# Seven-product feed-forward stage of a hybrid decoder layer: sample columns gated inside the PSUM bank, four down banks in the loops, casts and first sums reordered, output pieces moved to groups 19 and 20

## Chip, cores and metric

One core of a Trainium2 chip runs the whole kernel. The metric is device time in microseconds (us); lower is better. The kernel before takes 2521.41 us (median of 3 runs, 2520.0 to 2522.43).

Names of engines: PE is TensorE (matmuls), PEld its weight loads, DVE is VectorE, ACT is ScalarE, POOL is GpSimd, SP is SyncE, which issues most DMAs. L826 is line 826 of the kernel before.

## The reference

One decoder layer for 1024 prompt tokens and 64 sample tokens (8 sequences of 8), D_MODEL 1024, D_FF 2816, float32:

```python
x = x + 0.5 * gt1 * swiglu(modulate(x, norm_ffn1, sh1, sc1), ffn1_w_gu, ffn1_w_down)
x = x + gt2 * (parallel_heads(modulate(x, norm_mix, sh2, sc2)) @ w_out)
x = x + 0.5 * gt3 * swiglu(modulate(x, norm_ffn2, sh3, sc3), ffn2_w_gu, ffn2_w_down)
y = rms_norm(x, norm_final)
# swiglu(h, w_gu, w_down): gate, up = split(h @ w_gu, 2); (silu(gate) * up) @ w_down
```

The gates gt1 to gt3 have one value per channel for the prompt and one per channel and sequence for the samples. The change concerns the third line and the final norm.

## The kernel before

x stays in SBUF with channels on the partitions: 8 chunks of 128 channels by 1088 tokens, of which columns 1024 to 1087 are the samples. Each float32 product is made of three matmul passes over a high and a low part: high is the operand cast to fp32r (ACT), low is the operand less its high part (POOL or DVE). The last stage, `block_ffn` (L1510 to L2281), does the second feed-forward block. It works in two passes q over the tokens: tokens 0 to 543 (q = 0) and tokens 544 to 1087 (q = 1). A pass is two token tiles of 272 columns; the very last tile holds the 64 sample columns behind 208 prompt columns. Each pass goes over D_FF in 11 groups of two units (f chunks of 128 gate and 128 up channels), so groups are numbered G = 0 to 10 and 11 to 21.

The up and gate projections of a unit are a 2 by 2 block product done with seven block products in place of eight (named p1, p5, p6, p3, p7, p2, p4 in order of issue). Each product is 12 matmuls of 272 columns (L1802 to L1804) into PSUM banks 0 to 3. The weights need four sums of blocks first: S3 and S1 on POOL (L1679, L1685), S2 and S4 on DVE (L2085, L2091). Then ACT casts the high parts in two pieces (`up_high`, L1935, 2048 and 1536 columns) and POOL subtracts to get the low parts (`up_low`, L1690, four and three instructions of 512 columns). The x blocks have their sums too (T1 to T4), made once per pass.

After the products of a unit, DVE adds them up (`sum12`, `sum22`, `sum11`, L2095 to L2116), ACT applies silu (L1912 for the second token half, L1918 for the first), DVE multiplies (L2126, L2133), ACT casts the high part of the activation (`high`, L1922), DVE subtracts for its low part (`low`, L2121). Both units of a group being ready, PE does 16 down tiles v (8 output chunks for the second token half, v = 0 to 7, then 8 for the first, v = 8 to 15), 6 matmuls each (L487 to L489, called from `down`, L1807). A down tile goes to a bank of 4, 5, 6 in turn, and its wait on `dn_free` is for the DVE having read the tile three places before. DVE adds each tile to x with the gate (`summed`, L2144, which calls `add_gated_to`, L821):

```python
ins = dve.scalar_tensor_tensor(x[:, a:a + np_], bank[:, 0:np_], gate[:, 0:1], x[:, a:a + np_], ALU.mult, ALU.add)
if np_ < n:
    ins = dve.tensor_tensor(per_seq(scratch), per_seq(bank[:, np_:n]), over_tokens(gate[:, 1:9]), ALU.mult)
    dve.drain()
    dve.tensor_tensor(x[:, NP_TOK:T], x[:, NP_TOK:T], scratch, ALU.add)
```

The caller puts the increment of `dn_free` on the returned instruction. Only tiles v = 0 to 7 of pass q = 1 have sample columns. Among the tiles DVE also does S2 (after v = 8) and S4 (after v = 10) of the next group's second unit; S2 and S4 of its first unit stand between the two units (L2148).

Order of work is what each engine's program says: all five have a loop over groups and wait on one another's semaphores. ACT's `group` (L1941) does, for the second unit: take p1, silu, `up_high(G+1, 0, 0)`, high of the second half, silu, `up_high(G+1, 0, 1)`, high of the first half, then `up_high(G+1, 1, 0)` and `(1, 1)`. POOL's `group` does `up_lows(G, 1)`, S3, `dn_low(G)` (L1697, four instructions), S1, S3, `up_lows(G+1, 0)`, S1. SP's `next_group` (L1624) loads the next group's blocks as the products free them, and the down weights (1 MB) once the last down tile is through.

Before the first group, `first_sums` (DVE L2187, POOL L1724) and `first_highs` (ACT L1961) make the T sums and the high and low parts of the seven x blocks. In group 0 PE also takes the means of squares of the second pass's norm between down tiles (`early_means`, after v = 4, 7, 10, 13), for which ACT makes the squares (L764).

The final norm and output are cut into ten pieces of tokens (`Outputs`, L835). Per piece: PE transposes 8 blocks into two PSUM banks (L868), ACT squares and sums (L898), takes the root (L902, L904), DVE takes the reciprocal (L934), DVE scales and weights one half of the row (L942), ACT scales the other half (L930), POOL weights it (L954), SP writes it out. Pieces 0 to 3 (tokens 0 to 511, final since the first pass) use banks 4 to 7 and are all placed in group 21, after the second and sixth product of each unit. Before the down tiles of group 21 PE waits for these banks (L1893 to L1895).

## Time and profile before

| what | value |
|---|---|
| median of 3 runs | 2521.41 us |
| profiled execution, its own time | 2511.55 us |
| its span, first to last instruction | 2509.8 us |
| mean granted clock of TensorE | 0.979 |
| PE / PEld / DVE / ACT / POOL busy | 94% / 88% / 53% / 26% / 41% |
| `block_ffn`, first product to end of span | 1636.9 to 2509.8 us |
| a group of the first pass's loop (G = 1 to 9) | about 34.9 us |
| a group of the second pass's loop (G = 12 to 20) | about 37.8 us |
| group 0, group 10, group 11 (take of p1 to next) | 50.4, 51.3, 40.1 us |

The profiled execution lies 9.86 us below the median of the three runs. Busy time of PE comes from modelled ends of pipelined matmuls, so it is start-to-start steps and the idle times in brackets that show lost time.

### The profile page before, as it was taken

The page shows a single profiled execution, that of the slowest core. Times are in us where ns is not written, and L with a number is a line of the kernel's source. Part 1 is how long each engine was busy: PE and PEld are TensorE (multiplying, and loading weights), DVE is VectorE, ACT ScalarE, POOL GpSimd, SP SyncE. Part 2 cuts the span into 40 slices and gives each one's busy share as a digit, 9 for nine tenths or more (in the row PEclk, how much of TensorE's full clock was granted, in tenths as well). Part 3 has the DMA queues.
Part 4 walks back from the last instruction along what each step waited for, and adds up shares of the span by engine and source line. Part 5 has one row for each costly group of instructions (what it writes and reads, how often), then busy time and mean ns, then how long its engine had stood idle before and what let it go on. Part 6 is the DMA issues. An engine that isn't in the chain of part 4 may idle for free. (4 is left out here: it accounts for less than half of the span.)

```text
span 2509.8 us, 55182 instructions
## 1 busy us (share of the span) xinstructions
PE 2351.6 (94%) x22802; PEld 2209.7 (88%) x22802; DVE 1319.6 (53%) x2888; ACT 662.2 (26%) x1198; POOL 1032.9 (41%) x732
## 2 busy tenths in 40 slices
PE   6999999999999999999898899969999989999996
PEld 5899999999999999888488867969999978988986
DVE  4634444333444545343876752365656686666664
ACT  4100000000000323344611131254344343333335
POOL 2312121121221121111612044277878888778773
PEclk9999999999999999999899999989999999999998
DMA  9223221111101231011400025113322222322322
GB/s 331 85 101 100 67 84 51 50 47 37 50 21 46 72 95 56 26 35 39 140 4 5 5 64 154 44 51 101 92 87 87 85 76 76 92 75 84 92 70 86
DMA packets 214396, 185.91 MB, mean 74 GB/s; under 512 B 23787, under 2 KB 193436, under 8 KB 213843
## 3 DMA queue, kind: packets, MB, share of 16 engines
q1 hardware_dynamic: 213714, 181.36, 23.2%
q8 instruction: 122, 2.00, 0.3%
q10 hardware_dynamic: 144, 2.23, 0.2%
q14 instruction: 32, 0.25, 0.0%
q0 software_dynamic: 384, 0.07, 0.0%
HBM read 172.58 MB, written 11.34 MB: 73 GB/s over the span
## 5 line engine op out<-in xcount | busy, mean ns | idle before, releaser
L1690 POOL TENSOR_TENSOR f_up_lo<-f_up_raw,f_up_hi 128x512 fp32r<-128x512 f32 x308 | 392.8, 1312 | 146.8 <-ACT f_up_hi L1935 146.8
L487 PE MATMUL bank<-f_a_hi,f_dn_hi 128*128 128x272 f32 (+2 forms) x1232 | 393.4, 319 | 40.8 <-DVE f_scratch L829 20.8
L1802 PE MATMUL bank<-f_x_hi,f_up_hi 128*128 128x272 f32 x1232 | 361.9, 294 | 21.9 <-DVE f_x_lo L2162 10.3
L489 PE MATMUL bank<-f_a_hi,f_dn_lo 128*128 128x272 f32 (+2 forms) x1232 | 377.3, 306 | 0.0
L488 PE MATMUL bank<-f_a_lo,f_dn_hi 128*128 128x272 f32 (+2 forms) x1232 | 376.9, 306 | 0.0
L1804 PE MATMUL bank<-f_x_hi,f_up_lo 128*128 128x272 f32 x1232 | 359.3, 292 | 0.0
L1803 PE MATMUL bank<-f_x_lo,f_up_hi 128*128 128x272 f32 x1232 | 357.6, 290 | 0.0
L487 PE MATMUL bank<-hh,f_up_hi 128*128 128x368 f32 (+1 forms) x1008 | 331.0, 328 | 0.0
L489 PE MATMUL bank<-hh,f_up_lo 128*128 128x368 f32 (+1 forms) x1008 | 329.5, 327 | 0.0
L488 PE MATMUL bank<-hl,f_up_hi 128*128 128x368 f32 (+1 forms) x1008 | 329.1, 326 | 0.0
L487 PEld LDWEIGHTS bank<-f_a_hi,f_dn_hi 128*128 128x128 f32 x1232 | 233.3, 189 | 68.3 <-DVE f_scratch L829 33.3
L1101 POOL TENSOR_TENSOR f_up_lo<-f_up_raw,f_up_hi 128x2048 fp32r<-128x2048 f32 x22 | 101.8, 4626 | 408.1 <-DVE f_up_hi L1357 408.1
L1802 PEld LDWEIGHTS bank<-f_x_hi,f_up_hi 128*128 128x128 f32 x1232 | 234.8, 191 | 25.6 <-issue 13.4
L1370 DVE TENSOR_TENSOR f_prod<-f_silu,bank 128x368 f32<-128x368 f32 (+1 forms) x66 | 35.2, 533 | 394.4 <-PE bank L489 388.3
L1803 PEld LDWEIGHTS bank<-f_x_lo,f_up_hi 128*128 128x128 f32 x1232 | 235.3, 191 | 0.0
L1804 PEld LDWEIGHTS bank<-f_x_hi,f_up_lo 128*128 128x128 f32 x1232 | 234.7, 191 | 0.0
L488 PEld LDWEIGHTS bank<-f_a_lo,f_dn_hi 128*128 128x128 f32 x1232 | 234.0, 190 | 0.0
L489 PEld LDWEIGHTS bank<-f_a_hi,f_dn_lo 128*128 128x128 f32 x1232 | 233.6, 190 | 0.0
L502 DVE SCALAR_TENSOR_TENSOR x<-bank,mods,x 128x368 f32<-128x368 f32 (+1 forms) x280 | 157.8, 573 | 136.8 <-PE bank L489 124.7
L1306 ACT ACTIVATE f_silu<-bank 128x368 f32<-128x368 f32 (+1 forms) x66 | 31.3, 474 | 722.2 <-PE bank L489 717.2
L1935 ACT CAST f_up_hi<-f_up_raw 128x2048 fp32r<-128x2048 f32 x88 | 146.3, 1690 | 250.4 <-DVE f_up_raw L2091 228.2
L487 PEld LDWEIGHTS bank<-hh,f_up_hi 128*128 128x128 f32 x1008 | 189.1, 188 | 4.9 <-issue 4.9
(456 smaller groups left out, 4778.6 us busy)
## 6 DMA issues: line engine op xcount, KB each, us to landing
f_dn_raw<-in_ffn_w_down SPq DMA_DIRECT2D x33, 1024.0 KB, 4.9
f_up_raw<-in_ffn_w_gu SPq DMA_DIRECT2D x132, 256.0 KB, 2.9
f_up_raw<-in_ffn_w_gu SPq DMA_DIRECT2D x44, 512.0 KB, 5.0
ada<-in_w_ada SPq DMA_DIRECT2D x12, 1024.0 KB, 17.0
late<-in_w_ada SPq DMA_DIRECT2D x12, 1024.0 KB, 4.7
f_up_tmp<-in_ffn_w_gu SPq DMA_DIRECT2D x42, 256.0 KB, 3.8
w_in_raw<-in_w_in SPq DMA_DIRECT2D x16, 512.0 KB
gates<-in_w_ada SPq DMA_DIRECT2D x8, 1024.0 KB, 6.8
```

What stands on the lines that cost most here:

```text
L487: pe.matmul(out, wh, rh, start=(n == 0), stop=False)
L488: pe.matmul(out, wh, rl, start=False, stop=False)
L489: ins = pe.matmul(out, wl, rh, start=False, stop=(n == last))
L502: ins = dve.scalar_tensor_tensor(x[:, a:a + np_], bank[:, 0:np_], gate[:, 0:1], x[:, a:a + np_], ALU.mult, ALU.add)
L1101: pool.tensor_tensor(up_lo[j][:], up_raw[:], up_hi[j][:].bitcast(F32), ALU.subtract).then_inc(up_lo_done, 1)
L1306: act.activation(silu[u % 2][:, 0:n], k.psum[2 * (u % 2)][:, 0:n], ACT.Silu).then_inc(gate_free, 1)
L1370: dve.tensor_tensor(prod[u % 2][:, 0:n], silu[u % 2][:, 0:n], k.psum[2 * (u % 2) + 1][:, 0:n], ALU.mult).then_inc(up_free, 1)
L1690: ins = pool.tensor_tensor(up_lo[j][:, at], up_raw[j][:, at], up_hi[j][:, at].bitcast(F32), ALU.subtract)
L1802: pe.matmul(out, up_hi[j][:, w], x_hi[:, x], start=(c == 0), stop=False)
L1803: pe.matmul(out, up_hi[j][:, w], x_lo[:, x], start=False, stop=False)
L1804: ins = pe.matmul(out, up_lo[j][:, w], x_hi[:, x], start=False, stop=(c == KH - 1))
L1935: act.copy(up_hi[j][:, PARTS[part]], up_raw[j][:, PARTS[part]]).then_inc(up_hi_done[part], 1)
```

## The change

- `add_gated_to`: for a tile with sample columns, DVE first multiplies the 64 columns by their gates in place in the bank, then adds the 208 prompt columns to x, drains, and adds the 64 columns from the bank to x. The increment of `dn_free` is on this last instruction. The scratch tensor is no longer used here.
- Down tiles use four banks (4 to 7) in groups 1 to 9 and 11 to 20; three in groups 0, 10 and for v < 11 of group 21, then two.
- ACT's `group` casts the high part of the second half right after its silu and product, ahead of `up_high(G+1, 0, 0)`.
- Start of group 0: T3 and the low parts of B22 and B21 go from POOL to DVE; DVE's S2 and S4 of unit 1 go ahead of T1; ACT's order of casts changes and `take_p1(0, 0)` goes behind them. The last squares of the second pass's norm go ahead of `up_high(1, 1, ·)`.
- Output pieces 0 to 3: two in group 19 and two in group 20, one per unit, transposed after the second product. PE waits at the start of each of the two groups for all its down tiles to have been read, and before the down tiles of each for the rows of both pieces. ACT does a piece's squares and root after the high part of the unit's first half, DVE scales it there as well. Group 21 has no pieces in its products. In its down tiles DVE scales pieces 4, 5, 6 after v = 12, 14, 15 (was 11, 13, 15).
- SP issues the load of the final norm's weight ahead of the second pass's loads, not behind them.

```diff
-def add_gated_to(dve, k, i_gate, c, tile, bank, scratch):
+def add_gated_to(dve, k, i_gate, c, tile, bank):
...
+    if np_ < n:
+        dve.tensor_tensor(per_seq(bank[:, np_:n]), per_seq(bank[:, np_:n]), over_tokens(gate[:, 1:9]), ALU.mult)
     ins = dve.scalar_tensor_tensor(x[:, a:a + np_], bank[:, 0:np_], gate[:, 0:1], x[:, a:a + np_], ALU.mult, ALU.add)
     if np_ < n:
-
-        ins = dve.tensor_tensor(per_seq(scratch), per_seq(bank[:, np_:n]), over_tokens(gate[:, 1:9]), ALU.mult)
         dve.drain()
-        dve.tensor_tensor(x[:, NP_TOK:T], x[:, NP_TOK:T], scratch, ALU.add)
+        ins = dve.tensor_tensor(x[:, NP_TOK:T], x[:, NP_TOK:T], bank[:, np_:n], ALU.add)
...
-    def down_bank(v, last):
-        return k.psum[4 + (v % 2 if last and v >= KD else v % 3)]
+    def down_bank(v, banks):
+        return k.psum[4 + (v + 1) % 2] if banks == 2 else k.psum[4 + v % banks]
...
+            for sem in (sum_t1, sum_t3):
+                sp.wait_ge(sem, 2)
+            sp.dma_start(outputs.weight[:], ...
             with sp.Fori(0, NGRP - 1) as g:
                 next_group(g + NGRP, g + 1)
...
-            first_sums()
             with pool.Fori(0, NGRP - 1) as g:
                 group(g)
...
-                if last and v >= KD:
-                    pe.wait_ge(dn_free, ND * G + v - 1)
-                elif v >= 3:
-                    pe.wait_ge(dn_free, ND * G + v - 2)
+                if v >= banks:
+                    pe.wait_ge(dn_free, ND * G + v - banks + 1)
...
-            with pe.Fori(NGRP + 1, 2 * NGRP - 1) as g:
+            with pe.Fori(NGRP + 1, 2 * NGRP - 3) as g:
                 group(g)
+            for G in (2 * NGRP - 3, 2 * NGRP - 2):
+                pe.wait_ge(dn_free, ND * G)
+                for j in range(FC):
+                    for i in range(7):
+                        product(G, j, i)
+                        if i == 1:
+                            outputs.pe_tile(pe, FC * (G - 2 * NGRP + 3) + j)
+                outputs.set_free(pe, FC * (G - 2 * NGRP + 3) + 2, True)
+                for v in range(ND):
+                    down(G, v)
             G = 2 * NGRP - 1
-            pe.wait_ge(dn_free, ND * G)
...
-                    if i in (1, 5):
-                        outputs.pe_tile(pe, 2 * j + i // 5)
-            outputs.set_free(pe, 4)
-            pe.wait_ge(outputs.rows_done, outputs.EARLY)
-            pe.wait_ge(outputs.act_scaled, outputs.EARLY)
             for v in range(ND):
-                down(G, v, True)
+                down(G, v, 3 if v < KD + 3 else 2)
...
                 take_p1(G, 1)
-                swish2(G, 1)
+                second(G, 1)
                 up_high(G + 1, 0, 0)
-                high(G, 1, 1, gated2, high2)
                 swish1(G, 1)
...
                 if j == 0:
                     norms[1].squares(act, 2, 1)
                     norms[1].squares(act, 3, 0)
-            norms[1].squares(act, 3, 1)
+                    norms[1].squares(act, 3, 1)
...
+            for G in (2 * NGRP - 3, 2 * NGRP - 2):
+                n = FC * (G - 2 * NGRP + 3)
+                take_p1(G, 0)
+                second(G, 0)
+                dn_high(G)
+                first(G, 0)
+                outputs.squares(act, n)
+                take_p1(G, 1)
+                outputs.half_scale(act, n, outputs.bank(n, 0))
+                second(G, 1)
+                up_high(G + 1, 0, 0)
+                swish1(G, 1)
+                up_high(G + 1, 0, 1)
+                high(G, 1, 0, gated1, high1)
+                outputs.squares(act, n + 1)
+                outputs.half_scale(act, n + 1, outputs.bank(n + 1, 0))
...
             def first_sums():
...
+                sum_s2(0, 1)
+                sum_s4(1)
                 dve.wait_ge(norms[0].h_done, 2 * KD)
...
-                sum_s2(0, 1)
-                sum_s4(1)
+                x_low(X_B22, b22)
+                dve.tensor_tensor(t3, b22, b12_, ALU.subtract).then_inc(sum_t3, 1)
+                x_low(X_T3, t3)
+                x_low(X_B21, b21)
                 x_low(X_T4, t4)
...
+            for G in (2 * NGRP - 3, 2 * NGRP - 2):
+                for j in range(FC):
...
+                    low(G, j, 0, high1, act1_done)
+                    outputs.scaled(dve, FC * (G - 2 * NGRP + 3) + j)
+                    if j == 0:
+                        sum_s2(G + 1, 0)
+                        sum_s4(0)
```

## Rows read from the trace of the kernel before

**Rows 1.** The page: busy time of each engine and its share of the span.
```profile
PE 2351.6 (94%) x22802; PEld 2209.7 (88%) x22802; DVE 1319.6 (53%) x2888; ACT 662.2 (26%) x1198; POOL 1032.9 (41%) x732
```
**Rows 2.** Stretches: full clock, half clock, first-pass group, second-pass group; PE, PEld, DVE, ACT, POOL, PEclk.
```profile
2104.20:2116.20 12.00, 12.00 (x97) 12.00 (x97) 4.93 (x12) 3.79 (x7) 10.64 (x10) 1.00 0.55 178
2476.80:2479.80 3.00, 3.00 (x14) 3.00 (x15) 0.92 (x4) 0.00 (x0) 0.92 (x1) 0.50 0.27 77
1768.86:1803.73 34.87, 34.13 (x266) 33.43 (x266) 21.23 (x42) 14.45 (x17) 28.49 (x23) 1.00 0.30 91
2141.89:2179.72 37.83, 35.62 (x267) 33.73 (x266) 24.87 (x58) 11.89 (x15) 28.42 (x23) 1.00 0.27 82
```
**Rows 3.** PE's timeline, down tiles of group 12: start, duration, idle before and its releaser.
```profile
2123.78 0.39 PE L487 MATMUL bank<-f_a_hi,f_dn_hi 128*128 128x272 f32 x1 [0.16 <-issue]
...
2128.48 0.40 PE L487 MATMUL bank<-f_a_hi,f_dn_hi 128*128 128x272 f32 x1 [0.76 <-DVE f_scratch L829]
```
**Rows 4.** DVE's timeline, sample tiles v = 0, 1 and 5 of group 12.
```profile
2126.10 0.42 DVE L826 SCALAR_TENSOR_TENSOR x<-bank,mods,x 128x208 f32<-128x208 f32 x1
2126.44 0.21 DVE L829 TENSOR_TENSOR f_scratch<-bank,mods 128x64 f32<-128x64 f32 x1
2126.75 1.21 DVE L831 TENSOR_TENSOR x<-x,f_scratch 128x64 f32<-128x64 f32 x1
...
2128.52 0.67 DVE L831 TENSOR_TENSOR x<-x,f_scratch 128x64 f32<-128x64 f32 x1
...
2133.48 0.23 DVE L831 TENSOR_TENSOR x<-x,f_scratch 128x64 f32<-128x64 f32 x1
```
**Rows 5.** POOL's timeline in group 12: low parts, S1, and dn_low with its idle time.
```profile
2113.66 5.93 POOL L1697 TENSOR_TENSOR f_dn_lo<-f_dn_raw,f_dn_hi 128x512 fp32r<-128x512 f32 x4 [1.36 <-ACT f_dn_hi L1939]
...
2122.86 8.72 POOL L1690 TENSOR_TENSOR f_up_lo<-f_up_raw,f_up_hi 128x512 fp32r<-128x512 f32 x7 [0.77 <-ACT f_up_hi L1935]
2131.54 1.29 POOL L1685 TENSOR_TENSOR f_up_raw<-f_up_raw,f_up_tmp 128x512 f32<-128x512 f32 x1
```
**Rows 6.** DVE adds with one operand in a bank: nanoseconds, minimum/median/maximum of 44.
```profile
L2110 DVE TENSOR_TENSOR f_u2s<-f_u2s,bank x44: 428/430/433, 1658.1 to 2466.6; 128x272 f32<-128x272 f32 x44
```
**Rows 7.** DVE's second-half product in group 12, then ACT's timeline behind it.
```profile
2121.51 0.45 DVE L2126 TENSOR_TENSOR bank<-bank,f_vs 128x272 f32<-128x272 f32 x1
...
2120.87 1.91 ACT L1935 CAST f_up_hi<-f_up_raw 128x2048 fp32r<-128x2048 f32 x1 [0.60 <-POOL f_up_raw L1685]
2123.63 0.40 ACT L1918 ACTIVATE bank<-f_p1s 128x272 f32<-128x272 f32 x1 [0.57 <-DVE f_a_lo L2121]
```
**Rows 8.** What PE waited for between 1725 and 2010 (G = 2 to 9): us, times, longest.
```profile
PE bank L487 <- DVE x L826: 4.5, 16, 0.4
```
**Rows 9.** PE's timeline at the start of group 0 and at its last means of squares.
```profile
1636.88 0.56 PE L1802 MATMUL bank<-f_x_hi,f_up_hi 128*128 128x272 f32 x1 [5.60 <-DVE f_x_lo L2162]
...
1654.63 0.57 PE L1802 MATMUL bank<-f_x_hi,f_up_hi 128*128 128x272 f32 x1 [5.17 <-issue]
...
1691.69 0.57 PE L774 MATMUL bank<-f_sq,const 128*32 128x68 f32 x12 [6.22 <-ACT f_sq L764]
```
**Rows 10.** DVE's timeline at the start of group 0: one low part of an x block.
```profile
1643.71 1.28 DVE L2162 TENSOR_TENSOR f_x_lo<-f_x_raw,f_x_hi 128x1088 fp32r<-128x1088 f32 x1
```
**Rows 11.** PE's timeline of group 21: first product, third piece's transposes, first down tile.
```profile
2444.01 0.39 PE L1802 MATMUL bank<-f_x_hi,f_up_hi 128*128 128x272 f32 x1 [0.59 <-DVE x L826]
...
2460.59 1.06 PE L868 MATMUL bank<-const,x 128*128 128x128 f32 x8 [0.94 <-ACT x L930]
...
2476.54 0.59 PE L487 MATMUL bank<-f_a_hi,f_dn_hi 128*128 128x272 f32 x1 [6.46 <-DVE x L942]
```
**Rows 12.** The fourth output piece in group 21: ACT's squares and table load, DVE's scaling.
```profile
2472.18 0.60 ACT L898 ACTIVATE x<-bank 128x512 f32<-128x512 f32 x1
...
2473.86 1.28 ACT L904 ACT_TABLE_LOAD   x1
...
2475.74 0.75 DVE L942 SCALAR_TENSOR_TENSOR x<-bank,y_sums,y_weight 128x512 f32<-128x512 f32 x1
```

More of the change, by code:

```diff
@@ L869, in turn, with set_free @@
         return ins
-    def set_free(self, pe, j):
-        before = [i for i in range(j) if self.SETS[i] == self.SETS[j]]
+    def set_free(self, pe, j, every=False):
+        before = [i for i in range(j) if every or self.SETS[i] == self.SETS[j]]
         if before:
@@ L1655, in _ @@
             next_group(NGRP - 1, 0)
-            with sp.Fori(0, NGRP - 1) as g:
-                next_group(g + NGRP, g + 1)
             for sem in (sum_t1, sum_t3):
@@ L1661, in _ @@
                          ).then_inc(outputs.weight_in, 16)
+            with sp.Fori(0, NGRP - 1) as g:
+                next_group(g + NGRP, g + 1)
             outputs.sync(sp)
@@ L1805, in product, with down @@
                 ins.then_inc(prod_done[i], 1)
-            def down(G, v, last=False):
+            def down(G, v, banks=4):
                 a = SH * (1 - v // KD)
@@ L1820, in down @@
                 c = v % KD
-                three_passes(pe, down_bank(v, last)[:, 0:SH],
+                three_passes(pe, down_bank(v, banks)[:, 0:SH],
                              [(dn_hi[:, f, P * c:P * c + P], dn_lo[:, f, P * c:P * c + P], a_hi[:, f, a:a + SH], a_lo[:, f, a:a + SH])
@@ L1855, in early_means @@
                 for v in range(ND):
-                    down(0, v)
+                    down(0, v, 3)
                     if v in (4, 7, 10, 13):
@@ L2142, in unit, with summed, group @@
                 low(G, j, 0, high1, act1_done)
-            def summed(G, q, v, last=False):
+            def summed(G, q, v, banks=4):
                 dve.wait_ge(dn_mm, ND * G + v + 1)
-                return add_gated_to(dve, k, i_gate, v % KD, down_tile(q, v), down_bank(v, last), scratch[:, v % 2]).then_inc(dn_free, 1)
-            def group(G, q):
+                return add_gated_to(dve, k, i_gate, v % KD, down_tile(q, v), down_bank(v, banks)).then_inc(dn_free, 1)
+            def group(G, q, banks=4):
                 unit(G, 0)
@@ L2153, in group @@
                 for v in range(ND):
-                    summed(G, q, v)
+                    summed(G, q, v, banks)
                     if v == 8:
```

88 lines of the change are left out of this document (34 added, 54 removed).

## The prediction

> **What bounds the kernel now.** I read the page first: PE is busy 94% of the span and no other engine over 53% [rows 1]. So an edit pays only where PE's matmuls start late. The table of stretches gives the measure. At full clock 12.00 us hold some 95 starts, 0.126 us each; at a granted clock of 0.50 (1.2 of 2.4 GHz) 3.00 us hold 13, 0.23 each [rows 2]. A group has 14 x 12 + 16 x 6 = 264 matmuls, so its floor is 264 x 0.126 = 33.3 us. The first pass's loop takes 34.87 us, the second's 37.83 [rows 2]: 1.6 and 4.5 us lost per group. PE's timeline shows the losses at the down tiles: v = 0 starts 0.45 us behind its predecessor (0.16 idle and the predecessor's 0.29) where 0.126 is normal, so 0.3; then v = 4 idles 0.76 us for a DVE read of its bank [rows 3]. Each such late start costs 0.1 more, since its weight load isn't hidden. The sample tiles v = 0 to 7 are the second pass's extra.
>
> DVE's timeline says why [rows 4]. A sample tile is L826 (0.42), L829 (0.21), L831 (64 columns). L831 takes 1.21 and 0.67 us while POOL makes low parts, and 0.23 after. It reads two SBUF tensors; POOL's seven instructions take 8.72 / 7 = 1.25 us each [rows 5], and the first tiles come one per POOL instruction: L831 to L831 is 2128.52 - 2126.75 = 1.77, later ones 1.24. An add with one operand in a bank takes 428 to 433 ns in all 44 cases, beside POOL or not [rows 6]. So L831 waits for POOL's use of SBUF, and a bank operand frees it.
>
> **1. The sample tile, four banks, high part first (groups 11 to 18).** New tile: product in the bank, 0.14 to the next start (L829's 0.21 less the usual overlap of 0.07), L826's 0.42, drain 0.09 (L829 ends 2126.65, L831 starts 2126.75), add, 0.14 to the next start: 0.14 + 0.42 + 0.09 + 0.14 = 0.80 us against PE's 6 x 0.126 = 0.757. The add isn't in the trace; its bounds are 0.21 (L829, one bank operand) and 1.21 (L831 at worst). I take 0.21, since rows 6 show no waiting in this form. A page would have it dearer: the Trainium skill, "VectorE: DVE Perf Modes", section "The TRN2 errata", charges a bank source 120 cycles against 58, 65 ns more, by an estimate 0.93 us a tile and some 1 us more a group, 8 us in all. L829, from a bank, at 0.21 against L831 alone, from SBUF, at 0.23 shows no such surcharge [rows 4].
>
> The ACT move: the second half's product ends at 2121.96 [rows 7], so the high part starts at 2122.0, not behind the cast at 2122.7, and the first down tile needn't wait: 0.3 + 0.1 won. But the 1.91 us cast, which ran from 2120.87, now runs from 2122.3 to 2124.2; silu of the first half, at 2123.63, comes at 2124.1, and with it the second cast, the first half's high and low parts and DVE's first down tile: 2126.10 becomes 2126.55. PE's first tile starts at 2123.46; its fifth (v = 4) is due at 2126.49 and waits for the new release at the end of the add, 2126.55 + 0.14 + 0.42 + 0.09 + 0.21 = 2127.41: 1.0 + 0.1 lost. Then PE follows DVE's 0.80 to 0.81 for eight tiles: 8 x 0.05 = 0.4. POOL's low parts shift by 1.4 us with the cast and end, with S1's 1.29 [rows 5], near 2134.2, so DVE's S2 now falls beside POOL and v = 13 waits about 0.6. Loss 1.1 + 0.4 + 0.6 = 2.1 (bounds 1.3 and 3.0) against 4.5: -2.3 each (rounded), 8 x 2.3 = **-18** (-12 to -26). POOL waits 1.36 us for ACT before dn_low [rows 5] and starts about 0.85 later relative to the next group, so this cover just holds.
>
> **2. First pass (groups 1 to 9).** No sample tiles. The wait for DVE's read, 4.5 us in 16 cases over 8 groups [rows 8], is 0.56 a group, 0.76 with two late starts' extra. v = 4 is due at +3.03 and DVE comes 0.45 later than before, so that first wait stays at about 0.6; the one behind S2 goes, but S4 may now meet POOL. With v = 0's 0.4 won: -0.5 each (-0.2 to -0.9), 9 groups: **-4.5** (-2 to -8).
>
> **3. Start of group 0.** PE idles 5.6 us for the first low part and 5.17 us for T3's at 1654.63 [rows 9]. DVE gets three more instructions of 1088 columns, 1.28 us alone [rows 10], and POOL goes straight to the low weights. Two sums first (1.4 us, in an idle stretch of 0.8) delay T1 by 0.7, but without POOL beside them T1 and its successors take 1.28 to 1.3 each. I get the first product at 1636.4 and T3's low part at 1649 after alternating with four POOL instructions; `take_p1` after the casts lets p7 start at 1650, p2 waits for DVE's sum until 1652.5. That is **-3.7** (-1 to -5.5) at the group's seventh product. SP's down load waits for B21's low part, which DVE ends before T4's, at about 1650: ahead of p7's old start, so it isn't later, and the blocks queued behind it on SP aren't either. I take the point where p7 starts, less half of what p2's wait gives back; the low end is a first low part that only moves by the 0.5 us of the first product, the high end all of 5.17.
>
> **4. The last squares.** PE waited 6.22 us at 1691.69 [rows 9] and did its next 16 matmul steps at half clock (1.6 us). PE had come at 1691.69 - 6.22 = 1685.5. The squares need only the previous means, three down tiles earlier (3 x 0.757 + 0.1 = 2.4: 1683.1), and take ACT 1.1 us, so they are there by 1684.3. Next late is p1's copy, behind the roots' and a table load: 0.6. So -(6.22 + 0.3 + 1.6 - 0.6) = **-7.5** (-6 to -8.3).
>
> **5. Output pieces.** In group 21 go: the wait at the start (0.59 idle, 0.85 with restarts [rows 11]), 0.94 + 0.1 for piece 2's banks, 6.46 + 0.2 before the down tiles and 17 half-clock steps (17 x 0.1 = 1.8), in all 10.4. In come about 1.1, as DVE's first tile now lags. Transposes (0.95 a piece) move and cancel. In each of groups 19 and 20 come: 0.85 at the start; then piece n's squares and root, 3.3 us on ACT (table load 1.28 [rows 12]), hold DVE, which waits for the root before S2 and S4 of the next group, and these stand ahead of `sum12` of the second unit: p2 starts 1.9 late. After the unit's last high part ACT takes piece n + 1: 3.3, then DVE's reciprocal and 0.75 [rows 12], and PE's down tiles are held until both are done: from its first square to the end of that scaling the fourth piece took 2475.74 + 0.75 - 2472.18 = 4.3 us, and the high part ahead of it ends 2.4 us behind the products, so 6.7. The clock falls as it did after 6.46: 1.8. The tiles then have no backlog, 0.3. Sum 0.85 + 1.9 + 6.7 + 1.8 + 0.3 = 11.6 in place of 4.5: +7.1, twice +14.2. Net 14.2 - 10.4 + 1.1 = **+5** (-8 to +11; the low end if piece n + 1 hides). Table loads: the Trainium skill, "ScalarE: Activation LUTs", section "What ACT_TABLE_LOAD costs", adds a drain of 1.38 us to the load's 1.28. By it each group would lose 2.8 more, +5.5 in all. In rows 12 the root follows the load at once, so the sum leaves it out.
>
> **6. Rest.** The last group's fifth piece now pays a table load in the tail: **+0.8** (0 to 1.5). SP's weight load moves ahead of the loop: its waits are over before the first block is due, and 0.5 MB (the down load has 1 MB) finds the queue free: nothing; without this cover 1 to 2 us once.
>
> **Sum.** -18 - 4.5 - 3.7 - 7.5 + 5 + 0.8 = -27.9. Against the profiled execution 2511.55 becomes 2483.6; it lay 9.9 below the median of the runs, so against 2521.4 I expect **2493.5**.
>
> **Rivals.** (a) *The pieces hide*: ACT's last root comes before PE needs the banks. For it: PE needs only banks, and the transposes are 10 us earlier. Against: ACT's program has the squares behind the unit's last cast. It would save (6.7 + 1.8 - 1.4 for the backlog that returns) x 2 = 14: 2479. Chance 0.12.
> (b) *The add still waits for POOL*: x is in SBUF in both forms. Against: rows 6. Tiles stay at 1.24 and release the bank later; I work out -0.5 a group in place of -2.3: +14, 2508. Chance 0.12.
> (c) *Part 3 and 4's waits pass on* to POOL's low weights of the next unit, which follow their own casts: +9, 2502. Chance 0.1.
> (d) *Slower: the delayed cast chain becomes the bound.* Cast, low parts, S3, dn_low, S1 follow one another; the cast now starts 1.4 us later. dn_low ends at 2119.6 [rows 5], 4 us ahead of PE's tile at 2123.8, and POOL has 1.36 before it. Beyond 5.5 us of shift every down stage of 17 loop groups waits. A shift of 8 us costs 17 x 2.5 = 42: 2536. The row gives 1.4, so 0.04.
> (e) *The change doesn't do what it says*: the release behind the drain eats the fourth bank and pieces cost more, all parts cancelling: 2520. Chance 0.05.
>
> **Numbers.** The forecast has 0.57, its own range 2485 to 2502. 2479 to 2508 takes in (c), and the edges of (a) and (b). A measurement of this kernel can tell about 0.2%, 5 us, from no change: faster is the forecast and (a), (b), (c), 0.91; same is (e) 0.05; slower is (d) 0.04.
>
> **What would show it.** Right: L831's successor near 0.22 us at every tile; sample tiles 0.80 apart; second-pass groups near 35.5 us, first-pass 34.4; no PE wait over 1 us at the last means; PE idle near 6.5 us before the down tiles of both 19 and 20, with clock 0.5 behind it; group 21 without. Wrong: adds of 0.6 to 1.2 us (b); groups 19 and 20 under 40 us (a); PE waiting for dn_low (d).

## The result and the profile after

The changed kernel takes 2482.24 us (median of 4 runs, 2478.93 to 2486.84), the kernel before 2520.7 us beside it (4 runs, 2516.77 to 2522.43): 0.985 of the time, 95% interval 0.983 to 0.987. 2493.5 us were forecast, 2479 to 2508 the range. The profiled executions, 2511.55 and 2482.93 us, lie 28.6 us apart, for which 27.9 were forecast; the medians lie 38.5 apart, and the last experiment looks into why. One execution of the kernel of run 7, which took 2851.98 us at a mean granted clock of 0.745 where the others had 0.977 to 0.984, is left out of its median.

The page of the changed kernel, busy time by engine, beside [rows 1]:

```profile
PE 2331.9 (94%) x22802; PEld 2206.0 (89%) x22802; DVE 1294.8 (52%) x2891; ACT 665.2 (27%) x1202; POOL 1030.9 (42%) x726
```

The shares of busy time hardly move, though the kernel is 1.5% faster. The table of stretches shows where it gained: a first-pass group (G6), a second-pass group (G12), group 19, and the tail from the fifth output piece's transposes to the end. Columns as in [rows 2].

```profile
1859.55:1893.58 34.03, 33.56 (x267) 33.34 (x266) 20.24 (x42) 14.34 (x18) 29.48 (x23) 1.00 0.31 93
2082.75:2118.61 35.86, 34.23 (x266) 33.53 (x265) 23.73 (x58) 11.66 (x16) 28.48 (x23) 1.00 0.30 89
2334.48:2379.77 45.29, 37.07 (x282) 36.41 (x281) 23.69 (x62) 20.45 (x32) 28.02 (x23) 0.92 0.23 70
2453.23:2481.00 27.77, 13.21 (x86) 11.97 (x84) 11.38 (x23) 15.05 (x41) 6.92 (x5) 0.66 0.30 86
```

34.87 us have become 34.03 and 37.83 have become 35.86 [rows 2]; as means of several groups, 35.03 have become 34.13 and 37.92 have become 35.87. DVE's timeline of a sample tile in group 12, and the add's view by line (nanoseconds, minimum/median/maximum), beside [rows 4]:

```profile
2105.47 0.22 DVE L826 TENSOR_TENSOR bank<-bank,mods 128x64 f32<-128x64 f32 x1
2105.60 0.42 DVE L827 SCALAR_TENSOR_TENSOR x<-bank,mods,x 128x208 f32<-128x208 f32 x1
2106.09 0.22 DVE L830 TENSOR_TENSOR x<-x,bank 128x64 f32<-128x64 f32 x1
...
L830 DVE TENSOR_TENSOR x<-x,bank x88: 220/221/223, 2070.2 to 2452.8; 128x64 f32<-128x64 f32 x88
```

All 88 adds take 0.22 us, where L831 took 1.21 and 0.67 beside GpSimd; tiles start 0.76 to 0.78 apart. PE's remaining late starts in group 12 are two, v = 4 and one behind S2 (PE's timeline, then ACT's and POOL's, beside [rows 3, 5, 7]):

```profile
2106.37 0.39 PE L487 MATMUL bank<-f_a_hi,f_dn_hi 128*128 128x272 f32 x1 [0.92 <-DVE x L830]
...
2114.20 0.39 PE L487 MATMUL bank<-f_a_hi,f_dn_hi 128*128 128x272 f32 x1 [0.66 <-DVE x L827]
```
```profile
2100.90 0.39 ACT L1907 CAST f_a_hi<-bank 128x272 fp32r<-128x272 f32 x1 [0.85 <-DVE bank L2120]
2101.19 1.92 ACT L1920 CAST f_up_hi<-f_up_raw 128x2048 fp32r<-128x2048 f32 x1
```
```profile
2103.18 8.77 POOL L1686 TENSOR_TENSOR f_up_lo<-f_up_raw,f_up_hi 128x512 fp32r<-128x512 f32 x7 [2.54 <-ACT f_up_hi L1920]
2111.89 1.30 POOL L1681 TENSOR_TENSOR f_up_raw<-f_up_raw,f_up_tmp 128x512 f32<-128x512 f32 x1
```

GpSimd waits 2.54 us for the later cast, its S1 comes at 2111.89, and VectorE's S2 at 2112.05 takes 1.69 us beside it.

PE's timeline at the start of group 0, behind the last means, in group 19 and in the tail, beside [rows 9, 11]:

```profile
1638.18 0.56 PE L1785 MATMUL bank<-f_x_hi,f_up_hi 128*128 128x272 f32 x1 [4.92 <-DVE f_x_lo L2156]
...
1651.43 0.36 PE L1785 MATMUL bank<-f_x_hi,f_up_hi 128*128 128x272 f32 x1 [3.03 <-DVE f_x_lo L2156]
...
1654.76 0.36 PE L1785 MATMUL bank<-f_x_hi,f_up_hi 128*128 128x272 f32 x1 [1.58 <-DVE f_vs L2095]
...
1691.38 0.36 PE L1785 MATMUL bank<-f_x_hi,f_up_hi 128*128 128x272 f32 x1 [0.55 <-ACT f_p1s L1893]
...
2353.57 0.39 PE L1785 MATMUL bank<-f_x_hi,f_up_hi 128*128 128x272 f32 x1 [0.73 <-DVE f_vs L2095]
...
2363.75 0.59 PE L487 MATMUL bank<-f_a_hi,f_dn_hi 128*128 128x272 f32 x1 [6.89 <-DVE x L941]
...
2462.33 1.06 PE L867 MATMUL bank<-const,x 128*104 128x128 f32 x4 [1.78 <-DVE y_rows L941]
...
2466.54 0.84 PE L867 MATMUL bank<-const,x 128*96 128x128 f32 x3 [1.78 <-DVE y_rows L941]
```

The 6.22 us at the last means are gone (the 0.55 us are p1's copy of group 1); groups 19 and 20 each idle 6.9 us before their down tiles, as forecast, and the tail has two waits of 1.78 us where PE's timeline before had one:

```profile
2496.58 1.92 PE L868 MATMUL bank<-const,x 128*96 128x128 f32 x16 [1.78 <-DVE y_rows L942]
```

**How the experiments are read.** Ahead of VectorE's first product of the first norm (`xhat`) no instruction differs between any of the kernels here, yet it started between 1612.4 and 1625.7 us in the fourteen profiles. So beside the medians I give, from each profile, the time from that instruction to the end of the span, the *stage*: 896.4 us before, 865.6 after. "Second pass" is the mean of groups 12 to 17, "first pass" of groups 2 to 8, from p1's copy to the next group's; single groups of one kernel differ by steps of 0.4 to 0.5 us. Every ratio is to the kernel before, with its 95% interval.

### The profile page after: what moved, and what is told of

Its sections match the earlier page's. It is cut to its first block and busy times, and to the rows that moved or that the text cites. A ratio compares the mean times of both kernels' runs of the same rounds, so it can differ in the third digit from the quotient of the medians.

```text
span 2481.0 us, 55050 instructions
## 1 busy us (share of the span) xinstructions
PE 2331.9 (94%) x22802; PEld 2206.0 (89%) x22802; DVE 1294.8 (52%) x2891; ACT 665.2 (27%) x1202; POOL 1030.9 (42%) x726
## 5 line engine op out<-in xcount | busy, mean ns | idle before, releaser
L1686 POOL TENSOR_TENSOR f_up_lo<-f_up_raw,f_up_hi 128x512 fp32r<-128x512 f32 x308 | 401.2, 1342 | 151.3 <-ACT f_up_hi L1920 151.3
L487 PE MATMUL bank<-f_a_hi,f_dn_hi 128*128 128x272 f32 (+2 forms) x1232 | 384.9, 312 | 35.2 <-DVE x L941 13.8
L1785 PEld LDWEIGHTS bank<-f_x_hi,f_up_hi 128*128 128x128 f32 x1232 | 233.5, 190 | 28.4 <-issue 11.3
```

The lines of the kernel that those rows point to most:

```text
L487: pe.matmul(out, wh, rh, start=(n == 0), stop=False)
L1686: ins = pool.tensor_tensor(up_lo[j][:, at], up_raw[j][:, at], up_hi[j][:, at].bitcast(F32), ALU.subtract)
L1785: pe.matmul(out, up_hi[j][:, w], x_hi[:, x], start=(c == 0), stop=False)
```

## Experiments: the loops

**1. The samples' product in scratch again**, four banks and the new order kept.

```
-    if np_ < n: bank[:, np_:n] *= gate      (ahead of the prompts' line)
+    scratch = bank[:, np_:n] * gate         (behind it; releases the bank)
-    x[:, NP_TOK:T] += bank[:, np_:n]
+    x[:, NP_TOK:T] += scratch
```

> The changed kernel with the samples' gating as it was before: x += bank * gate for the prompts, product into a scratch tile in SBUF, then x += scratch; the bank is released by the product. Four banks, the new ScalarE order and the rest stay. Theory A (the 64-column add with both operands in SBUF waits for GpSimd): these adds show about 1.2 us while GpSimd makes low parts and 0.67 once more, as before the change, the sample tiles come 1.2 to 1.8 us apart there, and second-pass groups 12 to 17 take 37.3 to 37.8 us in place of 35.87; adding groups 11 and 18 to 20, some +14 to +18, about 2498 us. Theory B (the gain came from the fourth bank and the shorter tile, not from where the product lies): adds 0.23, groups 35.9 to 36.2, 2482 to 2486 us. The first pass has no sample tiles and stays at 34.1 in both.

Measured: 2502.98 us, 0.992 (0.990 to 0.994); stage 882.4; second pass 37.75, first 34.13. DVE's timeline, two sample adds of group 12:

```profile
2112.87 0.93 DVE L830 TENSOR_TENSOR x<-x,f_scratch 128x64 f32<-128x64 f32 x1
...
2114.37 0.67 DVE L830 TENSOR_TENSOR x<-x,f_scratch 128x64 f32<-128x64 f32 x1
```

Theory A: undoing this alone costs 16.8 us of stage. The 88 adds take 224 to 1353 ns, with a median of 665. With the add from scratch, the other two edits of the loops bring the second pass 0.2 us a group (37.92 to 37.75).

**2. Three down banks in the loops and in groups 19 and 20**, the rest kept.

```
-            def down(G, v, banks=4):
+            def down(G, v, banks=3):        (and so in VectorE's group)
```

> The changed kernel with three down banks in all loops and in groups 19 and 20; gating in the bank stays. Theory A: VectorE needs 0.77 us a tile and PE 0.757, so a bank more only moves the place of one wait by one tile: v = 3 now waits where v = 4 waited, 0.76 us longer. Each group of both passes costs 0.5 to 0.8 more (second pass 36.4 to 36.7 for 35.87, first 34.6 to 34.9 for 34.1), 17 to 19 groups, +9 to +14: about 2494 us. Theory B: with gating in the bank the fourth bank has no use, since VectorE follows PE at nearly its pace: under +0.1 a group, 2482 to 2484 us.

Measured: 2501.68 us, 0.992 (0.990 to 0.994); stage 882.6; second pass 36.47, first 35.35. PE's timeline in group 12, the wait at v = 3:

```profile
2118.98 0.40 PE L487 MATMUL bank<-f_a_hi,f_dn_hi 128*128 128x272 f32 x1 [1.67 <-DVE x L830]
```

1.67 us for 0.92 at v = 4: one tile of PE's more, as Theory A has it, but the first pass pays 1.2 us a group, over the 0.8 I had allowed, so the whole is +17 in the stage and +19 in the medians, not +9 to +14.

**3. ScalarE's old order**: cast first, then the second half's high part.

```
-                second(G, 1)
+                swish2(G, 1)
                 up_high(G + 1, 0, 0)
+                high(G, 1, 1, gated2, high2)
```

> The changed kernel with ScalarE's old order in the loops' groups: after the second silu first the 2048-column cast of the next weights, then the second half's high part. Theory A (the working of the prediction): what the move wins at v = 0 (0.3 idle and 0.1) it gives back at v = 4, since VectorE's first tile comes 0.45 us later behind the later chain; so undoing it changes a group by under 0.3 either way, v = 0 shows a wait of about 0.2 to 0.3 and the wait at v = 4 falls from 0.92 to about 0.5: 2479 to 2486 us. Theory B (the move is a gain of its own): +0.4 a group, 2489 us. Theory C (it is a loss of its own, the cast chain being late for all): -0.4 a group, 2475 us.

Measured: 2475.91 us, 0.981 (0.979 to 0.983); stage 853.1, 12.5 less than the changed kernel; second pass 34.32, first 34.06. Theory C: its 2475 us came out, but by 1.6 us a group of the second pass alone where it had 0.4 in both. PE's timeline at v = 0 of group 12, then DVE's first sample tile and S2, POOL's S1, and the table of stretches for the group:

```profile
2108.66 0.39 PE L487 MATMUL bank<-f_a_hi,f_dn_hi 128*128 128x272 f32 x1 [0.17 <-DVE f_a_lo L2116]
```
```profile
2110.99 0.22 DVE L826 TENSOR_TENSOR bank<-bank,mods 128x64 f32<-128x64 f32 x1
...
2117.56 0.73 DVE L2080 TENSOR_TENSOR f_up_raw<-f_up_raw 128x512 f32<-128x512 f32 x1
```
```profile
2116.46 1.28 POOL L1681 TENSOR_TENSOR f_up_raw<-f_up_raw,f_up_tmp 128x512 f32<-128x512 f32 x1
```
```profile
2089.11:2123.17 34.06, 33.89 (x266) 33.50 (x265) 21.85 (x58) 11.76 (x16) 28.48 (x23) 1.00 0.30 93
```

Counted from p1's copy (2089.11 here, 2082.75 in the changed kernel) the cast starts at 16.65 us (2105.76) for 18.44, VectorE's first tile at 21.88 for 22.72, S1 at 27.35 for 29.14. v = 0 pays 0.3 us, v = 4 waits for nothing, and S2, at 28.45, comes as S1 is ending and takes 0.73 us for 1.69, so its wait is gone too. With the old order group 12 is 0.8 us above PE's floor of 33.3, groups 12 to 17 on average 1.0.

**9. Of the loops' edits only the product in the bank**: three banks and the old order, by the diffs of 2 and 3 together.

> The changed kernel with three down banks and ScalarE's old order in the loops: of the loops' three edits only the product in the bank is left. Theory A (the gating in the bank carries the loops' gain, and four banks bring what a tile's head start is worth): the first pass is then the loop of the kernel before, 34.9 us a group (it has no sample tiles), the second pass takes 34.7 to 35.2 for 37.84 before and 34.2 with four banks; from the run with the old order and four banks +0.7 x 17 groups = +12, about 2488 us. Theory B (bank count matters only with the new order, whose first tile is late): 34.2 in both passes, 2476 to 2478 us. Theory C (the fourth bank carries the gain): second pass 36.5 or more, 2500 us.

Measured: 2493.58 us, 0.988 (0.986 to 0.990); stage 870.5; second pass 35.16, first 35.19. Theory A in its second pass; the first came out 0.3 us a group above its 34.9, and the whole 5.6 us higher than it said. Together:

| product in | banks | order | first pass | second pass | kernel |
|---|---|---|---|---|---|
| scratch | 3 | old | 35.03 | 37.92 | before |
| bank | 3 | old | 35.19 | 35.16 | 9 |
| bank | 4 | old | 34.06 | 34.32 | 3 |
| bank | 3 | new | 35.35 | 36.47 | 2 |
| scratch | 4 | new | 34.13 | 37.75 | 1 |
| bank | 4 | new | 34.13 | 35.87 | after |

In the second pass the product in the bank is worth 2.8 us a group with three banks and the old order, and 1.9 with four banks and the new order, so the edits don't simply add. The fourth bank brings 0.6 to 0.8, and the new order loses 1.6 with four banks and 1.3 with three. In the first pass the fourth bank brings 1.1 to 1.2, and the new order costs 0.1 to 0.2, no more than the steps between groups explain.

## Experiments: the start

**8. The start of group 0 as before** (`first_sums`, `first_highs` and GpSimd's part from the kernel before).

> The changed kernel with the start of group 0 as it was before: GpSimd makes T3 and the low parts of B22 and B21, VectorE the rest, ScalarE takes p1 between its casts. The unchanged kernels ahead of this stage end at times that lie up to 10 us apart in the profiles, so this is read from a matmul of the output projection's end to p1 of group 1's first unit. Theory A (the prediction: the move saves 3.7 us): that stretch is 3 to 5 us longer than in the changed kernel, about 2486 us. Theory B (the move saves more, since part 3 and part 4 together brought 13.0 in the profile against 11.7 forecast): 5 to 6 us longer, 2488. Theory C (all of the start's gain came from the squares moved to before the casts): 0 to 1 longer, 2483.

Measured: 2485.19 us, 0.987 (0.985 to 0.989); from `xhat` to p1 of group 1, 79.46 us for 75.45. PE's timeline, its two long waits:

```profile
1636.07 0.56 PE L1802 MATMUL bank<-f_x_hi,f_up_hi 128*128 128x272 f32 x1 [5.86 <-DVE f_x_lo L2173]
...
1652.86 0.57 PE L1802 MATMUL bank<-f_x_hi,f_up_hi 128*128 128x272 f32 x1 [6.23 <-DVE f_x_lo L2173]
```

+4.0 us, Theory A: the seventh product waits 6.23 us again for T3's low part. The whole stage read the same as the changed kernel's (865.8), as later stretches without a changed instruction came out shorter: groups 2 to 9 by 0.7 us, groups 12 to 17 by 1.6, and from group 19 to the end 1.5. So only the stretch is read, and the medians (+3.0 us) agree with it in direction only.

**10. The last squares behind both casts again.**

```
                     norms[1].squares(act, 3, 0)
-                    norms[1].squares(act, 3, 1)
+            norms[1].squares(act, 3, 1)
```

> The changed kernel with the last squares of the second norm back behind both casts of the next weights. Theory A (the prediction, 7.5 us): PE idles about 6 us before the last means in group 0's down tiles and makes its next steps at half clock; from p1 of group 0's first unit to p1 of group 1's it takes 44.5 to 47 us for 39.95, about 2488 us. Theory B (the squares hide now that the start of group 0 is earlier): a wait under 2 us, 41 to 42 us, 2483.

Measured: 2489.99 us, 0.987 (0.986 to 0.989). PE's timeline, the last means:

```profile
1686.17 1.13 PE L773 MATMUL bank<-f_sq,const 128*32 128x68 f32 x32 [6.22 <-ACT f_sq L763]
```

The same 6.22 us as in [rows 9]; group 0 takes 45.42 us for 39.95 and group 1, whose start had waited 0.55 for p1's copy, 34.48 for 32.12: +7.8, where the stage as a whole reads +6.6 (872.2) and the medians +7.8. Theory A.

## Experiments: the output pieces and the tail

**4. All four pieces in group 21 again**, with that group's instructions of the kernel before up to its down tiles. Behind them it keeps the changed kernel's bank count (three up to v = 10, then two) and places of VectorE's scalings.

> The changed kernel with the four early output pieces back in group 21, its instructions there as before the change; groups 19 and 20 are loop groups again. Theory A (by the changed kernel's profile): the two groups fall from 45.29 and 45.55 us to 35.9 to 36.5, and group 21 with the end goes from 55.68 back to some 64 (63.97 before), so -10 to -11: about 2472 us. Theory B (the sum of the prediction): the move costs 5 to 6 us, so 2476 to 2477. Theory C (the move pays, what groups 19 and 20 lose being lost in group 21 otherwise): 2487 us or more.

Measured: 2480.26 us, 0.983 (0.981 to 0.985); stage 859.1, 6.5 less than the changed kernel. Groups 19 and 20 take 35.86 and 36.51 us, as Theory A said, but from p1 of group 21 to the end it is 68.57 us, not 64. PE's timeline, first down tile and two transposes of the tail:

```profile
2446.94 0.59 PE L487 MATMUL bank<-f_a_hi,f_dn_hi 128*128 128x272 f32 x1 [6.46 <-DVE x L941]
...
2466.29 0.93 PE L867 MATMUL bank<-const,x 128*104 128x128 f32 x4 [1.78 <-DVE y_rows L941]
...
2470.36 1.91 PE L867 MATMUL bank<-const,x 128*96 128x128 f32 x8 [1.78 <-DVE y_rows L941]
```

The stretch up to the down tiles is the old one (6.46 us idle, [rows 11]); the excess lies in the tail, where this kernel kept the changed places of VectorE's scalings: two waits of 1.78 us though no table load falls there. So Theory A held in the two groups and missed the tail. The stage puts the cost of moving the pieces at 6.5 us, the medians at 2.0, around the number of Theory B and against Theory C. That number isn't the prediction's, though: its +5.8 for parts 5 and 6 was set against the old loop groups, and against the changed kernel's own it comes to 5.8 + 2 x 2.3 = 10.4. From group 19 to the end the run shows 5.6.

**6. VectorE's scalings in the tail where they were**, behind tiles 11, 13 and 15.

```
-                if v in (KD + 4, KD + 6, KD + 7):
+                if v in (KD + 3, KD + 5, KD + 7):
```

> The changed kernel with VectorE's scalings of pieces 4, 5 and 6 in the last group's down tiles after tiles 11, 13 and 15, as before the change, in place of 12, 14 and 15. Theory A (the later places make the transposes of pieces 8 and 9 wait, 1.78 us twice where the kernel before waited once): one of the two waits goes, and from piece 4's transposes to the end 27.8 us become 25.2 to 26, so -1.8 to -2.5: about 2480 us. Theory B (the table load of 1.28 us, now in piece 4's root, makes both waits): the earlier scaling holds VectorE instead while it waits for the root, the down tiles wait for their banks, and the time stays at 2481.5 to 2484.

Measured: 2483.38 us, 0.986 (0.984 to 0.987); stage 863.0, 2.6 less than the changed kernel; from p1 of group 21 to the end 52.49 us for 55.68. PE's timeline, the two waits:

```profile
2464.38 0.62 PE L867 MATMUL bank<-const,x 128*104 128x128 f32 x4 [1.25 <-DVE y_rows L941]
...
2467.53 0.72 PE L867 MATMUL bank<-const,x 128*96 128x128 f32 x5 [1.78 <-DVE y_rows L941]
```

Neither wait goes, one is shorter by 0.5. The medians show no gain (2483.38 for 2482.24); the profile shows 2.6 to 3.2, which the spread of the runs (3 to 8 us) can hide. Most of it is TensorE's clock. The table of stretches from the fifth piece's transposes to the end, in the kernel before, in run 9 (whose tail has the changed kernel's instructions) and in this run:

```profile
2486.32:2509.80 23.48, 10.28 (x86) 9.64 (x84) 11.01 (x22) 13.65 (x40) 6.96 (x5) 0.81 0.35 102
```
```profile
2466.73:2492.30 25.57, 10.47 (x86) 9.61 (x84) 11.38 (x23) 14.94 (x41) 6.96 (x5) 0.82 0.32 93
```
```profile
2456.11:2480.70 24.59, 10.31 (x86) 9.67 (x84) 11.30 (x23) 14.94 (x41) 6.96 (x5) 0.82 0.34 97
```

Run 9 has both waits of 1.78 us and takes 25.57 us at a clock of 0.82, where the changed kernel takes 27.77 at 0.66: 2.2 of its 4.3 us over before are transposes at half clock. At like clock the old places of the scalings are worth 25.57 - 24.59 = 1.0 us, under Theory A's 1.8 to 2.5. The lower clock may itself go with the waits: eight of the nine profiles with the changed places show 0.66 to 0.73 in this stretch, the five with the old places 0.81 to 0.85.

**5. One piece in each of groups 17 to 20.** Piece by piece: eight transposes behind the second product, p1 of the second unit copied ahead of the squares, VectorE's reciprocal between two sums of the second unit, its scaling behind them. All four pieces share one pair of banks, and PE's wait for its down tiles to be read comes after the second product, not at the group's start.

```
-            for G in (2 * NGRP - 3, 2 * NGRP - 2):          (two pieces each)
+            for G in range(2 * NGRP - 5, 2 * NGRP - 1):     (one piece each)
-                outputs.squares(act, n)
                 take_p1(G, 1)
+                outputs.squares(act, n)
-                outputs.squares(act, n + 1)
-                outputs.half_scale(act, n + 1, ...)
```

> The changed kernel with one output piece in each of the groups 17 to 20 in place of two in groups 19 and 20: its transposes after the first half's second product, ScalarE takes p1 of the second unit before the squares, VectorE's reciprocal lies between two sums of the second unit and its scaling behind them, so that all is done before PE needs the bank. ScalarE's order elsewhere is the changed kernel's. Theory A (what groups 19 and 20 lose is the piece that stands behind the last casts, 6.9 us of idle and the half clock behind it): groups 17 to 20 take 35.9 + 0.7 for eight transposes + 0.3 to 1 for a later silu behind the table load, 37 to 37.6 each, 149 to 150 in place of 35.87 + 36.5 + 45.29 + 45.55 = 163.2: -13 to -14, about 2468.5 us. Theory B (each piece costs its 4.7 us a group wherever it stands, ScalarE and VectorE being late for the unit): 40.5 each, no gain, 2482 us.

Measured: 2470.03 us, 0.980 (0.979 to 0.982); stage 852.2; the four groups take 36.75, 37.95, 37.96 and 39.21, 151.9 in all for 163.2. Theory A, at 11.3 us of its 13 to 14. PE's timeline in group 19:

```profile
2355.36 0.36 PE L487 MATMUL bank<-f_a_hi,f_dn_hi 128*128 128x272 f32 x1 [0.78 <-DVE f_a_lo L2117]
```

0.78 us of idle before the down tiles in place of 6.89, and the granted clock of the group is 1.00 in place of 0.92.

**7. All of it together**: 5, 3 (in all groups), 6, and a root of one column on ScalarE behind the last high part, to have the table in before the fifth piece.

> One output piece in each of groups 17 to 20 as in the run before the last, ScalarE's old order (cast of the next weights, then the second half's high part) in all groups, VectorE's scalings in the tail as before the change, and a root of one column on ScalarE behind the last high part, so that the table is loaded before piece 4 comes. Theory A (the parts add up): -13.5 for the pieces, -1.6 x 8 groups = -12.5 for the order as one run has shown, -4 for the tail: 2482.2 - 30 = 2452 us. Theory B (with the old order the silu of the second unit behind the table load makes groups 17 to 20 lose what they win): 2458 to 2462 us.

Measured: 2455.2 us, the median of five (2452.45 to 2463.01), 0.974 (0.973 to 0.976); stage 842.5. 2452 by Theory A, 2458 to 2462 by B: between them, and the profile shows what B feared. PE's timeline, first down tile of group 19, and ACT's ahead of it:

```profile
2357.18 0.36 PE L487 MATMUL bank<-f_a_hi,f_dn_hi 128*128 128x272 f32 x1 [1.97 <-DVE f_a_lo L2120]
```
```profile
2351.98 0.69 ACT L929 ACTIVATE x<-bank,y_sums 128x512 f32<-128x512 f32 x1 [2.46 <-DVE y_sums L933]
2352.68 1.28 ACT L1901 ACT_TABLE_LOAD   x1
2353.98 0.38 ACT L1901 ACTIVATE bank<-bank 128x272 f32<-128x272 f32 x1
```

ScalarE waits 2.46 us for the reciprocal, and the scaling and the table load then stand ahead of the silu. In the tail the first of the two waits falls to 0.42 us, and from the fifth piece's transposes to the end it takes 23.77 us for run 6's 24.59, both at a clock of 0.82: the table load is worth 0.8 us there.

**11. The same with the table load and the reciprocal taken off that chain.**

```
                 outputs.squares(act, n)
+                act.activation(outputs.col(n, 1), outputs.col(n, 1), ACT.Silu)
                 outputs.half_scale(act, n, outputs.bank(n, 0))
...
+                outputs.inverse(dve, piece)
+                sum12(G, 1)
                 sum22(G, 1)
                 gated_second(G, 1)
                 sum11(G, 1)
+                outputs.scaled_row(dve, piece)
```

> The best kernel so far with three edits in groups 17 to 20: a Silu of one column behind the root, so that the table comes back while ScalarE waits anyway; VectorE's reciprocal ahead of the second unit's sums; its 512-column scaling in front of the wait for ScalarE's high part. Theory A (PE's 1.97 us of idle before the first down tile come from the scaling and the table load ahead of the second unit's silu, which starts 1.6 us late): that wait falls to 0.2 to 0.6 and each of the four groups from 37.1 to 35.4 to 35.8 us, some -6 in all: about 2450 us. Theory B (VectorE is what is late, S4 ending at 16.4 us of the group beside GpSimd): the wait stays above 1.2 us, 36.6 or more a group, 2454 to 2457 us.

Measured: 2447.6 us (5 runs, 2444.8 to 2456.19), 0.971 (0.969 to 0.973), 1.4% under the changed kernel; stage 830.2. ACT's timeline in group 19, PE's first down tile, and the group:

```profile
2336.19 1.28 ACT L903 ACT_TABLE_LOAD   x1
2337.49 0.29 ACT L903 ACTIVATE y_sums<-y_sums 128x1 f32<-128x1 f32 x1
2337.80 1.28 ACT L2057 ACT_TABLE_LOAD   x1
2339.09 0.20 ACT L2057 ACTIVATE y_sums<-y_sums 128x1 f32<-128x1 f32 x1
2339.33 0.69 ACT L929 ACTIVATE x<-bank,y_sums 128x512 f32<-128x512 f32 x1
2341.00 0.38 ACT L1901 ACTIVATE bank<-bank 128x272 f32<-128x272 f32 x1 [0.98 <-DVE bank L2104]
```
```profile
2344.21 0.36 PE L487 MATMUL bank<-f_a_hi,f_dn_hi 128*128 128x272 f32 x1 [0.44 <-DVE f_a_lo L2121]
```
```profile
2322.86:2358.75 35.89, 35.08 (x274) 34.39 (x274) 23.22 (x60) 16.91 (x27) 28.48 (x23) 1.00 0.28 88
```

Theory A. The four groups take 35.90, 34.96, 35.89 and 35.95 us: 142.7, where the same four take 34.19 + 35.28 + 45.98 + 44.38 = 159.8 in run 3.

## Experiment: the kernel before, once more

> The kernel before, profiled a second time. Its first profiled execution took 2511.55 us, below all its other runs (2513.8 to 2528.7). In ten profiles of changed kernels the first VectorE product of the first norm, ahead of which no instruction differs, started between 1612.4 and 1625.7 us; in the first profile of the kernel before at 1613.4. Theory A (the kernel before is the same from there on, and its profiled execution only had an early start of this stage): from that instruction to the end 896 us again, within 2, and the start lies 2 to 12 us later. Theory B (the stage itself takes longer in most executions than in the first profile, which would explain why the medians show 38.5 us gained where the profiles show 28.6): 899 to 906 us in this stage.

Measured: 2519.57 us, span 2517.8. DVE's timeline, the stage's first instruction, in the first profile of the kernel before and in this one:

```profile
1613.44 2.87 DVE L798 TENSOR_TENSOR f_raw_h<-x,bank 128x272 f32<-128x272 f32 x8 [0.24 <-PE bank L792]
```
```profile
1618.83 2.87 DVE L798 TENSOR_TENSOR f_raw_h<-x,bank 128x272 f32<-128x272 f32 x8 [0.24 <-PE bank L792]
```

The stage takes 2517.8 - 1618.83 = 899.0 us for 896.4: 5.4 of the 8.0 us lie ahead of it, 2.6 in it. The start is Theory A's, the stage lies just outside its 2 us and at the edge of Theory B. So the first profile caught an early start. The stage accounts for 31 to 33 of the 38.5 us of the medians (896.4 or 899.0 less 865.6). The other 6 or so lie ahead of it, in work that the change doesn't touch; that they are chance is likely from the 13 us over which its start is spread, but not shown.

## Why the prediction was right

The mechanisms held in the main, and the range holds the median. That the sum was right to 0.7 us in the profile is partly luck: the stage gained 30.8 us (896.4 - 865.6) for 27.9, and the changed kernel's stage happened to start 2.0 us later. Of the stage's gain 16.8 us come from part 1, 7.2 from groups 2 to 9, 13.0 from the start with group 1 and 0.5 from group 10, less 2.5 and 4.3 for parts 5 and 6; that makes 30.7. The median lies 11 us under the forecast, because that was set from a profiled execution that I took to lie 9.9 below the runs for good; the changed kernel's profile lies at its own median.

- **Part 1**, forecast -18: group 11 gave 40.07 - 37.48 = 2.6, groups 12 to 17 2.05 each, group 18 1.3, into which part 5's wait at the start of group 19 falls (0.6); without it 16.8 together. The steps held: add 0.22 (0.21 forecast), tiles 0.77 apart (0.80, though its terms add up to 0.79), a wait at v = 4 of 0.92 idle (1.1 with its restart), one behind S2 of 0.66 (0.6). Rival (b), the add waiting on although x is in SBUF, is refuted by 88 adds. On the Trainium skill's "VectorE: DVE Perf Modes", "The TRN2 errata": its surcharge for a bank source (120 cycles against 58, by an estimate 65 ns) doesn't show in the runs, where 64 columns take 0.22 us from a bank (L826, L830) and 0.23 from SBUF [rows 4]. What the working did not draw out is its own balance: it priced the later cast at 1.1 for v = 4 and 0.6 for S2, against 0.4 won at v = 0. By its times v = 4 would have waited 0.15 with the old order too (2126.96 for 2126.81), so it says that the move of the high part loses some 1.2 us a group by itself. Run 3 shows 1.6. My expectation there, under 0.3 either way, ignored that working and was wrong. GpSimd's wait before dn_low, which was to shrink by 0.85, is 0.4 us where it was 1.36, and PE never waits for these low parts: rival (d) is out, though with little to spare.
- **Part 2**, forecast -4.5: groups 2 to 9 gave 278.7 - 271.5 = 7.2. The step that failed is "that first wait stays at about 0.6": only one wait a group is left (0.47 us in G6), and by the table above the fourth bank alone brings 1.1 to 1.2.
- **Parts 3 and 4**, forecast -3.7 and -7.5: runs 8 and 10 give 4.0 and 7.8 back. Both mechanisms and both sizes held. From `xhat` to p1 of group 2 the stretch fell by 120.57 - 107.57 = 13.0, so rival (c), the waits passed on, is out.
- **Part 5**, forecast +5: groups 19 and 20 grew by 7.4 and 6.95 us over before, or 5.8 and 5.4 without the two pieces' transposes, which the forecast counts as cancelling (7.1 each forecast). The wait before the down tiles was 6.89 (6.7 forecast), at the start 0.61 and 0.60 (0.85 with its restart forecast), p2's only 0.73 for 1.9: VectorE's S2 and S4 behind the root cost less than I had. In group 21 the stretch up to the fifth piece's transposes fell from 40.5 to 27.9 us, 12.6, with 3.2 of it transposes that moved; the other 9.4 are the forecast's 10.4 - 1.1. With group 18's 0.6 the net is +2.5.
- **Part 6**, forecast +0.8 (0 to 1.5): from those transposes to the end 23.5 us became 27.8, +4.3. This is the term that failed. I priced the table load, which held (0.8 us, run 7 against run 6), and passed over the new places of VectorE's scalings, though the diff shows them: a piece's transposes need the banks of the piece three before, and a scaling set one tile later holds them. By run 6 against run 9 the places cost 1.0 us at like clock. The largest share, 2.2 us, is TensorE's clock in this stretch, 0.66 for 0.81, which I didn't foresee either. Parts 5 and 6 together, +6.8 for +5.8, are right by chance.
- The table load: on the Trainium skill's "ScalarE: Activation LUTs", "What ACT_TABLE_LOAD costs", the drain of 1.38 us shows in none of the rows here. In run 11 the root follows a load at 2336.19 + 1.28 by 0.02 us, and the next load follows the root.

Rival (a), the pieces hiding, was wrong for this kernel, as the program order had it; runs 5 and 11 show that another order hides most of them. Against groups 12 to 16 of run 11, 34.13 us each, 142.7 - 4 x 34.13 = 6.2 us are left for four pieces. Of these 3.2 are transposes: in the changed kernel those of piece 1 start at 2381.09 and the next product at 2381.88. Rival (e), all parts cancelling, is out by the table of the loops and the runs of the start.

In the tail either cause alone keeps a wait: with late scalings and no table load (run 4) both 1.78 us waits stay, with early scalings and the load (run 6) the first is 1.25, and with neither (run 7) 0.42. The changed bank count of group 21 costs at most 0.3 us, as run 7 keeps it and its tail takes 23.77 us for 23.48 before. Open is why the clock in the tail is lower with the late places; and each of these prices rests on one profile of each kernel.

## What to carry to other kernels

Price each moved instruction by itself and by both sides, even inside an edit that gains: the change's 1.5% hid a move that loses 0.3 to 0.5% (6.3 us by the medians, 12.5 by the stage) and a placement of the pieces that loses about as much, and without them, with the table loads and the reciprocal placed better, the same ideas give 2.9%. An engine's side work (a root, a table load, a scaling) belongs where that engine waits anyway, in front of what it waits for; one piece per group there costs 1.5 us, half of it transposes, and two in a group, one of them behind the last cast, cost 9.4 us. When the work ahead moves by more than what is measured, anchor the profile at the first instruction of the stage.

## What the runs showed of the hardware

When the stage starts goes with TensorE's granted clock in stretches ahead of it, which the change doesn't touch. The stretch 1020 to 1240 us in the profiles of run 4 (late start of the stage, 1625.7) and run 5 (early, 1612.8), from the table of stretches:

```profile
1020.00:1240.00 220.00, 212.96 (x1343) 167.93 (x1341) 105.88 (x324) 102.23 (x291) 51.21 (x41) 0.90 0.18 60
```
```profile
1020.00:1240.00 220.00, 210.57 (x1362) 166.59 (x1360) 111.10 (x341) 107.81 (x307) 55.11 (x45) 0.95 0.18 60
```

With the same instructions, more of the stretch was granted 1.2 GHz in run 4, and 17 fewer VectorE instructions were reached. The difference, 0.05 of 220 us, is 11 us of full clock, for 12.9 us between the two starts. What sets the clock there isn't shown.

VectorE's 512-column subtraction of two SBUF tensors (S2) takes 0.73 us at the end of GpSimd's S1 (run 3) and 1.69 beside it (the changed kernel). On 64 columns the sum with both operands in SBUF took 224 to 1353 ns (run 1), and with one operand in a bank 220 to 223 ns, beside GpSimd or not (88 each); the product in the bank took 222 to 233.
